# Value sums of the sample group spread over 40 attention steps, and early probability blocks turned by products with the identity, in a hybrid decoder trunk

## The reference

```python
# prompt group, 8 heads of 64, blocks of 128 queries
sc = jnp.einsum('bqhd,bkhd->bhqk', q_i, k).astype(jnp.float32) * scale
sc = sc + (f_i[..., :, None] - f_cum[..., None, :])
sc = jnp.where(k_pos[None, :] <= q_pos[:, None], sc, -jnp.inf)
p = jax.nn.softmax(sc, axis=-1).astype(v.dtype)
return jnp.einsum('bhqk,bkhd->bqhd', p, v)
# sample group: past pages and the new token
p = jax.nn.softmax(jnp.concatenate([s_past, s_new], axis=-1), axis=-1).astype(v.dtype)
o = (jnp.einsum('bhqk,bkhd->bqhd', p[..., :p_len], v_past.astype(v.dtype))
     + jnp.einsum('bhqk,bkhd->bqhd', p[..., p_len:], v))
```

## Time and profile before

| | us |
|---|---|
| median of 3 runs | 2940.92 |
| lowest, highest | 2938.22, 2946.79 |
| profiled execution, its own time | 2951.03 |
| its span, first to last instruction | 2949.1 |
| attention, first mask product to first projection unit | 371.89 to 729.53 |
| mean granted clock of PE | 0.936 |

### The profile page before, as it was taken

One profiled execution on the slowest core, in us unless ns is written; L12 is line 12 of the kernel. 1 busy time (PEld: TensorE's weight loads), 2 busy tenths in 40 slices (PEclk: granted clock), 3 DMA queues, 4 the chain that ended last, 5 costly groups with the idle time before them and its releaser, 6 DMA issues.

```text
span 2949.1 us, 41762 instructions
## 1 busy us (share of the span) xinstructions
PE 2742.0 (93%) x16732; PEld 2596.6 (88%) x16732; DVE 1298.0 (44%) x1540; ACT 730.1 (25%) x1116; POOL 890.5 (30%) x556
## 2 busy tenths in 40 slices
PE   4999899998989999999997898888989999999996
PEld 2999877557979999999997798778979999999995
DVE  5189986222263333333335400487263333333336
ACT  3321134333131211111112322254131111111111
POOL 4276641000132333333332311240233333333330
PEclk9999956996999999999998999968999999999998
DMA  3397666992111111111111211420201111111111
GB/s 129 101 329 252 233 208 233 386 374 80 43 36 36 55 45 50 43 50 43 50 48 36 90 43 56 115 93 31 95 29 50 43 50 43 50 43 50 43 46 58
DMA packets 121642, 286.61 MB, mean 97 GB/s; under 512 B 20117, under 2 KB 21014, under 8 KB 121018
## 3 DMA queue, kind: packets, MB, share of 16 engines
q1 hardware_dynamic: 84474, 170.34, 16.3%
q10 hardware_dynamic: 36736, 113.72, 12.4%
q0 software_dynamic: 320, 1.05, 0.1%
HBM read 262.86 MB, written 22.18 MB: 97 GB/s over the span
## 4 chain that ended last, share of the span: by engine, by line
PE 75%; DVE 11%; DMA 5%; issue 3%; ACT 2%; POOL 1%; SPq 1%; ACTq 0%; POOLq 0%; DVEq 0%
PE G L644 63%; PE M L836 2%; PE G L800 2%; DMA XT<-in_ck 2%; DVE KTMP L1589 2%; DVE QT L1556 2%; PE M L777 1%; DVE XT L1575 1%; DMA HF<-in_cv 1%; PE G L825 1%; DVE KT L1533 1%; PE G L689 1%; POOL WLO L1962 1%; DMA XT<-in_xs 1%; DVE KT L1519 1%
## 5 line engine op out<-in xcount | busy, mean ns | idle before, releaser
L1962 POOL TENSOR_TENSOR WLO<-WRAW,WHI 128x1024 fp32r<-128x1024 f32 x192 | 465.0, 2427 | 1418.3 <-ACT WHI L1361 831.3
L644 PE MATMUL G<-HHI,WHI 128*128 128x344 f32 x3408 | 731.1, 323 | 21.1 <-issue 7.3
L644 PE MATMUL G<-HLO,WHI 128*128 128x344 f32 x3408 | 727.8, 322 | 0.0
L644 PE MATMUL G<-HHI,WLO 128*128 128x344 f32 x3408 | 723.6, 321 | 0.0
L644 PEld LDWEIGHTS G<-HHI,WHI 128*128 128x128 f32 x3408 | 577.6, 190 | 24.1 <-issue 16.5
L644 PEld LDWEIGHTS G<-HLO,WHI 128*128 128x128 f32 x3408 | 580.8, 190 | 0.0
L644 PEld LDWEIGHTS G<-HHI,WLO 128*128 128x128 f32 x3408 | 572.1, 189 | 0.0
L1780 DVE TENSOR_TENSOR XT<-XT,G 128x1032 f32<-128x1032 f32 x192 | 236.0, 1230 | 405.5 <-PE G L644 389.3
L644 PE MATMUL G<-HIDH,WHI 128*128 128x344 f32 x1056 | 224.7, 321 | 14.0 <-issue 14.0
L1361 ACT ACTIVATE WHI<-WRAW 128x1024 fp32r<-128x1024 f32 x108 | 112.4, 1056 | 492.6 <-PE G L644 492.6
L644 PE MATMUL G<-HIDH,WLO 128*128 128x344 f32 x1056 | 225.6, 322 | 0.0
(11 more groups left out here) (289 smaller groups left out, 3025.8 us busy)
## 6 DMA issues: line engine op xcount, KB each, us to landing
WRAW<-in_w ACTq DMA_DIRECT2D x192, 512.0 KB, 3.6
XT<-in_ck SPq DMA_DIRECT2D x218, 256.0 KB, 4.1
HF<-in_cv SPq DMA_DIRECT2D x152, 256.0 KB, 7.2
XT<-in_cv SPq DMA_DIRECT2D x104, 256.0 KB, 7.0
HF<-in_ck SPq DMA_DIRECT2D x38, 256.0 KB, 3.0
XT<-in_xp SPq DMA_DIRECT2D x2, 4096.0 KB, 16.8
x_scr<-XT SPq DMA_DIRECT2D x1, 4128.0 KB, 11.7
XT<-x_scr SPq DMA_DIRECT2D x1, 4128.0 KB, 13.6
```

Of the source, the lines that this page charges most:

```text
L644: mm = pe.matmul(out[:, c], w, x[:, c * TC:(c + 1) * TC], start=first and n == 0, stop=last and n == 2)
L1962: TT(WLO[:, s], WRAW[:, s], WHI[:, s].bitcast(F32), ALU.subtract).then_inc(w_lo, 1)
```

## The change

The table `VALUES` is made by another rule. Before, from step 22 on, two groups were added at each step, so that 64 were reached at k = 53. Now the number due rises evenly, so that 64 is reached at k = 61 (`V_LAST` is 62): 40 steps with one or two groups, 1.6 on average. No step takes groups of two sequences; the eighth group of a sequence ends its step's share. `BATCH_MASKED` and `BATCH_SUMMED` follow from the table: the seven masks move from k = 25, 29, ... 49 to k = 26, 31, ... 56, the sums to one step after each.

In `turns`, the steps k < 22 form the product of the probability block with the identity in place of `pe.transpose`. `transpose` and `matmul` are given the same operands and the same place in PSUM.

```diff
 V_FIRST = EARLY + 2
-V_STEP = 2
-VALUES = [min(GROUPS, max(0, (_k + 1 - V_FIRST) * V_STEP)) for _k in range(HB * NB)]
+V_LAST = HB * NB - 2
+VALUES = []
+for _k in range(HB * NB):
+    _had = VALUES[-1] if VALUES else 0
+    _due = max(0, -(-(_k + 1 - V_FIRST) * GROUPS // (V_LAST - V_FIRST)))
+    VALUES.append(min(_due, _had - _had % 8 + 8, GROUPS))
 BATCH_MASKED = {min(_k for _k in range(HB * NB) if VALUES[_k] >= 8 * (_b + 1)): _b for _b in range(B - 1)}
 BATCH_SUMMED = {_k + 1: _b for _k, _b in BATCH_MASKED.items()}
...
                     for q in range(r * 4, min(r * 4 + 4, qb + 1)):
-                        mm = pe.transpose(G[n % 2][:, 2, (q % 4) * P:(q % 4 + 1) * P], SC[k % 2][:, q * P:(q + 1) * P],
-                                          ident)
+                        turned, block = G[n % 2][:, 2, (q % 4) * P:(q % 4 + 1) * P], SC[k % 2][:, q * P:(q + 1) * P]
+                        if k < V_FIRST:
+                            mm = pe.matmul(turned, block, ident, start=True, stop=True)
+                        else:
+                            mm = pe.transpose(turned, block, ident)
                     mm.then_inc(pt_psum, 1)
```

## The result

The changed kernel takes 2932.47 us (median of 8 runs, 2923.12 to 2934.60, but for one disturbed run of 5294.51 that the comparison leaves out), against 2945.53 for the kernel before (8 runs, 2933.33 to 2956.52). The ratio is 0.9949, with a 95% interval of 0.9924 to 0.9973: 15 us faster, give or take 7 (the two medians lie 13.1 apart). Forecast were 2914 us and 27 us gained. The profiled execution has a span of 2931.0 us against 2949.1.

The account below looks back on a forecast made before the run. In attention, PE at half clock was taken to bound the early and last steps, page transfers the value steps between. Terms -19, -5 and -3 sum to -27 us, giving 2914 us for the median, range 2900 to 2940.

Parts of the forecast that it names:

- Pages and bound of B: Attention steps 22 to 61: page waits fall from 11 to 2 us, PE sets the pace, 191 us if the clock holds.
- Values spread, -19: Steps 22 to 61: spreading the value groups cuts 209.9 us to 191, if the clock holds; ends -10 and -21.
- Rival B: Steps 22 to 61: 1.6 groups a step no longer hold the clock, 3.5 us per half-clock step; chance 0.07.
- Last steps and tail, -5: Steps 62, 63 and tail: the clock outlives the last values; full clock gives -7, a fall in the tail -3.
- Identity products, -3: Steps below 22: real products lift the clock to full two thirds of the time, 116.6 us; ends -15 and +21.
- Rival A: Steps below 22: identity products don't lift the clock, +21 in place of -3, 2938 us; chance 0.15, dear form 0.02.
- Rival C: Steps 22 to 61: uneven pages still set the pace, -10 in place of -19, 2923 us; chance 0.10.

Follow-up runs that it names:

- e13: e1 with the value sums' products 64 columns wide instead of one; 2927.26 us, ratio 0.9942 to the kernel before.
- e1: The change with every turn a transposition, so only the values spread; 2932.50 us, ratio 0.9956 to the kernel before.
- e2: The kernel before with only the identity products in steps below 22; ratio 1.0016.
- e3: The kernel before with each block in steps below 22 transposed twice; profiled attention 346.7 us against 357.6, no ratio given.
- e11: e3 run again, this time timed against the kernel before; ratio 0.9986.
- e6: The full change run a second time, unaltered; ratio 0.9935 to the kernel before.
- e10: e1 with the spread ending four steps earlier, at step 57 (1.78 groups a step); ratio 0.9912 to the kernel before.
- e5: Spread values, with each block below step 22 transposed twice in place of identity products; ratio 0.9942 to the kernel before.
- e4: The full change with identity products in all 64 steps; ratio 1.0025 to the kernel before.
- e14: The full change with the value sums' products 64 columns wide; 2921.98 us, ratio 0.9941 to the kernel before.
- e9: e1 run a second time unchanged; 2932.19 us, ratio 0.9942 to the kernel before.
- e7: e1 with the third value sum moved one step later, from step 37 to 38; profiled attention 350.6 us, no ratio given.

## Why the prediction was right and wrong

**Pages and bound of B: right.** The waits for pages went from 18.8 us to none, and the 40 steps' floor at full clock is as worked out: 191 us forecast, 192.96 measured in e13, which enters step 22 at half clock.

**"Values spread, -19": wrong in size, -9.3** (e1 -10.4). The step that failed is its condition, "if the clock holds". It held in 181.9 of 200.7 us; of the other 18.7 us 13.7 lie in the three falls, and without falls (e13) those three pairs of steps are 6.5 us shorter. In its place the runs showed falls behind the one-column value sums, which widening them removes (e13), and, as a reading, behind the 8-row forget sums. Where no fall came, in e13, the term was -17. I took the long stretch at 0.99 in the earlier trace rows for a property of the work; e2, e3 and e11 run the same work at the old table and fell 5 and 10 times. The profile before showed one of several courses, and so did the one after: the same kernel's second execution (e6) took 195.0 us in B, -14.9.

**Rival B: the fall, but not the cause.** It made the thinner mixture of 1.6 groups the cause and 3.5 us a step the price. Measured were three pairs of steps, at 1.6 to 3.2 us a pair. Against the mixture speak e10 and e13, the one-column sums are charged by e13. I had seven `value_sum` in the change's list and priced them at nothing, since none was added; their neighbours changed.

**"Last steps and tail, -5": -2.6**, just short of the end of -3, a fall in the tail: C's clock was 0.62. With the clock held longer (0.67 and 0.68) it was -4.4 in e5, -4.3 in e6 and -4.7 in e13.

**"Identity products, -3": the clock rose as forecast, but for another cause, and the size hangs on the execution.** +2.6 here, -5.2 in e6, +7.1 in e2, +0.9 in e4, -2.2 in e14, all within the ends of -15 and +21, and +0.6 on average. The price at full clock, 4.75 us a step, was met by the nine steps at 0.84 (4.71). Two thirds at full clock was too much: 31 to 50 us of 115 to 127. The seven steps at 0.55 took 7.05 us each, 1.17 more than before; the forecast was 0.96 more for the mean step of 4.5 blocks, which is 1.07 for the 5 blocks that these seven turn. PE stood for 4.4 of these 49.35 us. The cause that the text gave, that the products are real ones, is refuted by e3: more instructions in a row do it. Rival A did not come: the clock did rise, and a product was two instructions.

**Rival C: no.** No wait for pages is left.

**The sum.** -19, -5 and -3 became -9.3, -2.6 and +2.6: -9.3 in the profiled attention against -27. The measured 15 us lie between. The second execution of the change (e6) has an attention of 333.2 us, 24.4 below the profile before, at a ratio of 0.9935: near the forecast, but by -14.9, -5.2 and -4.3, and set against a profiled execution of the kernel before that lies 10 us above the median. That 2932 us lies inside the forecast's 2900 to 2940 says little for the mechanism, since that range leaves falls in B out and reaches 2940 by a rival in A. How the 15 us split isn't known, since only profiled executions show stretches, and these vary in A and in the unchanged code. I subtracted the whole forecast from the median although the half clock that the change mends need not be as long in each run: the kernel before scatters over 2927 to 2966 us here, one run of 3079.79 left out.

## What to carry to other kernels

Before a forecast rests on a clock that "holds", look for the few thin instructions between the dense ones (here one column wide, and perhaps those of 8 rows), and check a second execution: a clock at 1.00 in one profile can be one of several courses. A one-column product can be made wide for nothing where its cost is the instruction and not the columns; behind 64 columns the clock did not fall here, though elsewhere in the stretch it still could. When a stretch stands at half clock, try the same instruction twice before another instruction, as a test of the cause (timed, it gained nothing here), and ask first which engine is next: above DVE's pace of 4.7 us a step the clock bought nothing.

## What the runs showed of the hardware that was not expected

- Sixty-three extra columns in a value sum cost nothing: step 57, which has one, took 6.36 us in the changed kernel (669.77 to 676.13) and in e13 (662.92 to 669.28), both at 2.4 GHz; steps 32 and 47 likewise, 5.2 and 6.0 us in both. None of 25 wide sums without 8-row products in their step was followed by a fall of the clock; 35 of 89 narrow ones were.
- Falls stood at the same places in two executions of one program (e1 and e9; e3 and e11, counted from step 22), 0.5 us apart at most. They moved when B was entered otherwise: the changed kernel had three falls, its second execution, which entered B at full clock, two, at steps 28 and 38. e7 had two falls before its work differs from e1's, where e1 had none, with the clock risen 0.7 us sooner in step 22.
- PE can be busy in 95% of a stretch at 1.2 GHz (113.95 of 119.87 us in A before) without the clock rising, for 120 us; in e10, by the same code in A, it rose for 10.2 us, and A took 120.0 us all the same.
- Transpositions issued twice raise the clock as identity products do.
